# Last two expert quads' weight homes exchanged, last down weights in column halves, first unit of block 2 in row halves, router chain reordered

## The reference, cut to what matters

```
g_sel = argmax(xn @ w_router_group + b)             # 1 group of 4
top_v, top_i = top_k(e_logits of that group, 2)      # 2 of its 8 experts
gates = g_prob * softmax(top_v)
hdn = ragged_dot(xs, w_e_in, sizes)                  # 32 experts, 1024 x 512
act = silu(gate_h) * up_h
ys = ragged_dot(act, w_e_out, sizes)                 # 256 x 1024
h = h + scatter_add(ys * gates)
...
h = rms_norm(h, norm_f_g); xn = rmsnorm(h, ln1)      # block 2
proj = xn @ w_in_2                                   # first columns used: v_a, v_c, f, then q_a, k_a
```

## Time and profile before

| | us |
|---|---|
| three runs | 919.08, 919.75, 921.74; median 919.75 |
| the profiled execution, time | 920.25 |
| its span | 918.4 |
| TensorE busy | 836.1 (91%) |
| VectorE, ScalarE, POOL busy | 493.2, 385.9, 96.9 |
| DMA | 217.55 MB, mean 237 GB/s |

### The profile page before, as it was taken

One profiled execution on the slowest core, in us unless ns is written; L12 is line 12 of the kernel. 1 busy time (PEld: TensorE's weight loads), 2 busy tenths in 40 slices (PEclk: granted clock), 3 DMA queues, 4 the chain that ended last, 5 costly groups with the idle time before them and its releaser, 6 DMA issues.

```text
span 918.4 us, 14705 instructions
## 1 busy us (share of the span) xinstructions
PE 836.1 (91%) x5971; PEld 693.7 (76%) x5971; DVE 493.2 (54%) x768; ACT 385.9 (42%) x526; POOL 96.9 (11%) x115
## 2 busy tenths in 40 slices
PE   4989999999999996875678899999999899999996
PEld 4989789989997532322332599999997799999995
DVE  5898577764564411101110476555776577677584
ACT  5333454455332321111110665456554366556462
POOL 4322000111000000000000401122160000000000
PEclk9999999999999998988898999999999999999998
DMA  8665555234689999999999985434536446646511
GB/s 279 226 194 183 184 184 184 92 126 151 234 334 400 390 423 421 422 421 422 422 421 408 270 182 184 175 105 180 144 132 231 159 138 215 197 141 227 180 46 46
DMA packets 93647, 217.55 MB, mean 237 GB/s; under 512 B 13919, under 2 KB 44765, under 8 KB 81305
## 3 DMA queue, kind: packets, MB, share of 16 engines
q1 hardware_dynamic: 92905, 215.32, 64.9%
q10 hardware_dynamic: 576, 1.18, 0.4%
q0 software_dynamic: 112, 0.30, 0.3%
HBM read 215.44 MB, written 1.34 MB: 236 GB/s over the span
## 4 chain that ended last, share of the span: by engine, by line
PE 71%; DMA 13%; DVE 9%; ACT 3%; issue 2%; SPq 1%; POOL 0%; DVEq 0%; ACTq 0%
PE ps L858 17%; PE ps L859 16%; PE ps L860 16%; DMA moe_ring<-in_w_expert_in 12%; PE ps L1281 6%; PE ps L1197 6%; DVE w_lo L1658 3%; PE ps L1229 1%; PE ps L1219 1%; PE ps L1013 1%; PE ps L1023 1%; PE ps L1169 1%; DMA h_tok<-in_x 1%; SPq L724 1%; PE ps L1061 1%
## 5 line engine op out<-in xcount | busy, mean ns | idle before, releaser
L860 PE MATMUL ps<-x_hi,w_lo 128*128 128x256 f32 x664 | 189.1, 285 | 0.0
L860 PEld LDWEIGHTS ps<-x_hi,w_lo 128*128 128x128 f32 x664 | 128.7, 194 | 0.0
L1658 DVE TENSOR_TENSOR w_lo<-stage,w_hi 128x2048 fp32r<-128x2048 f32 (+1 forms) x44 | 101.8, 2354 | 25.3 <-ACT w_hi L1362 23.5
L858 PE MATMUL ps<-x_hi,w_hi 128*128 128x256 f32 x360 | 104.7, 291 | 4.7 <-DVE w_lo L1658 3.9
L859 PE MATMUL ps<-x_lo,w_hi 128*128 128x256 f32 x360 | 103.2, 287 | 0.0
L1362 ACT ACTIVATE w_hi<-stage 128x2048 fp32r<-128x2048 f32 (+1 forms) x44 | 79.2, 1849 | 55.7 <-PE ps L860 49.9
L858 PE MATMUL ps<-x_hi,w_odd 128*128 128x256 f32 x312 | 89.8, 288 | 1.3 <-DVE x_lo L1649 1.3
L859 PE MATMUL ps<-x_lo,w_odd 128*128 128x256 f32 x312 | 88.9, 285 | 0.0
L860 PE MATMUL ps<-x_hi,w_odd 128*128 128x256 f32 x312 | 88.9, 285 | 0.0
L858 PE MATMUL ps<-x_hi,w_lo 128*128 128x256 f32 x304 | 86.5, 285 | 0.0
L859 PE MATMUL ps<-x_lo,w_lo 128*128 128x256 f32 x304 | 86.0, 283 | 0.0
(11 more groups left out here) (386 smaller groups left out, 1914.7 us busy)
## 6 DMA issues: line engine op xcount, KB each, us to landing
stage<-in_w_in SPq DMA_DIRECT2D x23, 2048.0 KB, 8.1
moe_ring<-in_w_expert_in SPq DMA_DIRECT2D x44, 1024.0 KB, 18.3
moe_ring<-in_w_expert_out SPq DMA_DIRECT2D x20, 1024.0 KB, 15.7
stage_b<-in_w_up SPq DMA_DIRECT2D x12, 1024.0 KB, 7.6
stage<-in_w_down SPq DMA_DIRECT2D x11, 1024.0 KB, 5.2
stage<-in_w_up SPq DMA_DIRECT2D x10, 1024.0 KB, 9.6
up_odd<-in_w_expert_in SPq DMA_DIRECT2D x8, 1024.0 KB, 20.2
down_odd_a<-in_w_expert_out SPq DMA_DIRECT2D x6, 1024.0 KB, 21.7
```

The costliest lines, as they stand in the source:

```text
L858: mm(out, still[0], moving[0], start=first, stop=False)
L860: return mm(out, still[1], moving[0], start=False, stop=last)
L1658: tt(lo[:, cols], staged(n)[:, cols], hi[:, cols].bitcast(fp32), ALU.subtract).then_inc(lo_ready, 1)
```

## The change

1. Homes: up(6, half 1) goes to `up_odd` and up(7, half 0) to `moe_up[1]`, and they change places in SP's queue; down(7) goes to `up_odd`'s home. The semaphores that TensorE waits for follow.
2. Down(7) is loaded in two column halves, eight DMAs of 0.5 MB with 2 KB pieces, each half with a semaphore; the last quad's down products wait for their half. The last scatter goes (tile 0, half 0), (1, 0), (0, 1), (1, 1).
3. `vvf` is loaded in two row halves, six DMAs, and SP also waits for the last `up_full` ahead of it. POOL splits row half 0, ScalarE and VectorE row half 1; ScalarE's cast for it stands ahead of the norm, its first cast of `qka` behind the norm's `raw_hi`. `kbvb`'s load no longer waits for the last `down_b`, the bias loads do.
4. `route()`: the rank product of tile 0 and the first half of tile 1's logits ahead of the wait for the last quarter of h_tok; transposes copied in two halves; one rank product after `choose(1)` ahead of the signal; the sums for `most` after it, with a signal of their own; `residual`s moved. ScalarE scales tile 0 before it waits for the last quarter; POOL adds EPS ahead.

```diff
@@ -282,7 +282,7 @@
     u = units[s["unit"]]
-    s["pool"] = u["name"] == "vvf" or s["half"] == 1 and (u["name"], u["i"]) in POOL_SPLITS
+    s["pool"] = (u["name"], s["half"]) == ("vvf", 0) or s["half"] == 1 and (u["name"], u["i"]) in POOL_SPLITS
...
@@ -607,15 +608,20 @@
            for x in (down_odd_a, down_odd_b) for n in range(2)]
-down_last = [moe_up[1][:, j, :, :].rearrange("p k c -> p (k c)").rearrange("p (f c) -> p f c", c=D) for j in range(QUAD)]
+up_odd_home = [up_odd[:, 0, :, :], up_odd[:, 1, :, :], up_odd_c[:, :, :], up_odd_d[:, :, :]]
+down_last = [x.rearrange("p k c -> p (k c)").rearrange("p (f c) -> p f c", c=D) for x in up_odd_home]
...
-    if last and half == 1:
-        return up_last[j]
-    if (p, half) == (1, 0):
-        return up_odd[:, j, :, :] if j < 2 else (up_odd_c, up_odd_d)[j - 2][:, :, :]
-    return moe_up[half][:, j, :, :]
+    if (p, half) == (0, 0):
+        home = moe_up[0][:, j, :, :]
+    elif (p, half) == ((0, 1) if last else (1, 0)):
+        home = up_odd_home[j]
+    elif last and half == 1:
+        home = up_last[j]
+    else:
+        home = moe_up[1][:, j, :, :]
+    return home
...
@@ -655,9 +661,11 @@
             dst = staged3(n, WIDTH[name])
-            eng.dma_start(dst[:, :, 0:256], w_in2[:, :, VA0:VA0 + 256]).then_inc(first_in, 16)
-            eng.dma_start(dst[:, :, 256:384], w_in2[:, :, VC0:VC0 + 128]).then_inc(first_in, 16)
-            eng.dma_start(dst[:, :, 384:388], w_in2[:, :, FB0:FB0 + 4]).then_inc(first_in, 16)
+            for half in range(2):
+                ks = slice(half * KT // 2, (half + 1) * KT // 2)
+                eng.dma_start(dst[:, ks, 0:256], w_in2[:, ks, VA0:VA0 + 256]).then_inc(first_in[half], 16)
+                eng.dma_start(dst[:, ks, 256:384], w_in2[:, ks, VC0:VC0 + 128]).then_inc(first_in[half], 16)
+                eng.dma_start(dst[:, ks, 384:388], w_in2[:, ks, FB0:FB0 + 4]).then_inc(first_in[half], 16)
...
@@ -717,17 +725,24 @@
+    def up_landed(p, half, last):
+        if last and (p, half) == (1, 1):
+            return up_last_in
+        if last:
+            return moe_in[(4, 1)[p]]
+        return moe_in[4 if (p, half) == (1, 0) else half]
...
             src = w_up[half][:, e, :, :].rearrange("p e k n -> p (e k n)")
-            eng.dma_start(expert_up(p, half, j, last).rearrange("p k n -> p (k n)"), src).then_inc(up_last_in if last else moe_in[4 if (p, half) == (1, 0) else half], 16)
-
-    def load_down(q, p, experts=range(QUAD), last=False):
+            eng.dma_start(expert_up(p, half, j, last).rearrange("p k n -> p (k n)"), src).then_inc(up_landed(p, half, last), 16)
+
+    def load_down(q, p, experts=range(QUAD)):
...
             src = w_down[:, e, :, :].rearrange("p e f n -> p (e f n)")
-            eng.dma_start(expert_down(p, j, last).rearrange("p f n -> p (f n)"), src).then_inc(down_last_in if last else moe_in[2 + p], 16)
+            eng.dma_start(expert_down(p, j).rearrange("p f n -> p (f n)"), src).then_inc(moe_in[2 + p], 16)
...
@@ -744,10 +759,18 @@
         load_down(QUADS - 2, 0)
-        next_quad(QUADS // 2 - 2, 1)
+        eng.wait_ge(up_a, QUADS - 2 + it0)
+        load_up(QUADS - 2, 0, 1, last=True)
+        eng.wait_ge(up_full, QUADS - 2 + it0)
+        load_up(QUADS - 1, 1, 0, last=True)
+        eng.wait_ge(down_b, QUADS - 2 + it0)
...
         eng.wait_ge(up_full, QUADS - 1 + it0)
-        load_down(QUADS - 1, 1, last=True)
+        for half in range(2):
+            for j in range(QUAD):
+                cols = slice(half * BANK, (half + 1) * BANK)
+                e = QUADS * QUAD - QUAD + j
+                eng.dma_start(expert_down(1, j, True)[:, :, cols], w_down[:, e, :, cols]).then_inc(down_last_in[half], 16)
...
@@ -788,25 +811,24 @@
...
     for n in range(units_one, len(units)):
-        if n == units_one + STAGES:
+        if n == units_one + STAGES + 1:
             eng.wait_ge(down_b, passes * QUADS)
-        if n == units_one + STAGES + 1:
...
             eng.wait_ge(y_b, passes * QUADS)
+            eng.wait_ge(up_full, passes * QUADS)
...
@@ -1089,31 +1111,35 @@
-        residual(0, 0)
...
         eng.wait_ge(sel_ready, 1)
+        mm(ps[:, 1, 0:32], tri[:, 0:P], chosen[:, 0, :], start=True, stop=True).then_inc(rank_full, 1)
+        wait_read(eng, "at", "xt", 1)
+        router_logits(3, 1, range(0, 4))
...
         eng.wait_ge(h_ready, 4)
-        mm(ps[:, 2, 0:32], tri[:, 0:P], chosen[:, 0, :], start=True, stop=True).then_inc(rank_full, 1)
...
             last = eng.transpose(ps[:, 0, k * P:(k + 1) * P], interleaved(h_tok, 1, 1)[:, k, :], ident[:, :])
-        last.then_inc(xt_full, 1)
-        residual(0, 1)
-
-        wait_read(eng, "at", "xt", 1)
-        eng.wait_ge(xt_copied, 1)
-        router_logits(3, 1).then_inc(lg_full, 1)
+            if k % 2 == 1:
+                last.then_inc(xt_full, 1)
+        mm(ps[:, 2, 0:32], tri[:, P:S], chosen[:, 0, :], start=True, stop=False)
+
+        residual(0, 0)
+        for half in range(2):
+            eng.wait_ge(xt_copied, half + 1)
+            last = router_logits(3, 1, range(4 + 2 * half, 6 + 2 * half))
+        last.then_inc(lg_full, 1)
...
             gather_of(half, 0)
+        residual(0, 1)
...
         eng.wait_ge(sel_ready, 2)
-        mm(ps[:, 2, 32:64], tri[:, P:S], chosen[:, 0, :], start=True, stop=False)
-        mm(ps[:, 2, 32:64], tri[:, 0:P], chosen[:, 1, :], start=False, stop=True)
-        mm(ps[:, 2, 64:96], tri[:, P:S], chosen[:, 0, :], start=True, stop=False)
-        mm(ps[:, 2, 64:96], tri[:, P:S], chosen[:, 1, :], start=False, stop=True).then_inc(rank_full, 1)
+        mm(ps[:, 2, 0:32], tri[:, 0:P], chosen[:, 1, :], start=False, stop=True).then_inc(rank_full, 1)
+        for t in range(NT):
+            last = mm(ps[:, 3, 0:32], tri[:, P:S], chosen[:, t, :], start=(t == 0), stop=(t == 1))
+        last.then_inc(rank_full, 1)
...
@@ -1185,17 +1212,21 @@
             eng.wait_ge((xg_a, xg_b)[half], it + 1)
-            if half == 0:
+            if half == 0 and not final:
                 eng.wait_ge(moe_in[(0, 4)[p]], it * 32 + (64, 32)[p])
+            elif half == 0:
+                eng.wait_ge(moe_in[1], (r + 1) * (64 * (QUADS - 1)))
...
                 eng.wait_ge(up_last_in, r * 64 + 64)
+            elif tail:
+                eng.wait_ge(moe_in[4], it * 32 + 64)
...
                     last = mm(ps[CAP * j:CAP * (j + 1), 2, :], xg[p][:, k, CAP * j:CAP * (j + 1)],
-                              expert_up(p, half, j, final)[:, kk, :], start=(k == 0), stop=(k == KT - 1),
+                              expert_up(p, half, j, tail)[:, kk, :], start=(k == 0), stop=(k == KT - 1),
...
@@ -1207,13 +1238,13 @@
             eng.wait_ge(xg_b, it + 2)
-        if final:
-            eng.wait_ge(down_last_in, r * 64 + 64)
-        elif p == 0:
+        if p == 0:
             eng.wait_ge(moe_in[2], it * 32 + 64)
-        else:
+        elif not final:
...
         for half in range(2):
+            if final:
+                eng.wait_ge(down_last_in[half], r * 64 + 64)
...
@@ -1222,14 +1253,14 @@
         eng.wait_ge(spread_ready, it + 1)
-        for t in range(NT):
-            for half in range(2):
-                if t == 0:
-                    eng.wait_ge((y_a, y_b)[half], it + 2)
-                last = mm(ps[:, 4 + 2 * t + half, :], spread[:, t * P:(t + 1) * P],
-                          y_slots[:, half * BANK:(half + 1) * BANK], start=False, stop=False,
-                          skip_group_check=True)
-            last.then_inc((scat0, scattered)[t], 1)
+        for t, half in ((0, 0), (1, 0), (0, 1), (1, 1)) if final else ((0, 0), (0, 1), (1, 0), (1, 1)):
+            if t == 0:
+                eng.wait_ge((y_a, y_b)[half], it + 2)
+            last = mm(ps[:, 4 + 2 * t + half, :], spread[:, t * P:(t + 1) * P],
+                      y_slots[:, half * BANK:(half + 1) * BANK], start=False, stop=False,
+                      skip_group_check=True)
+            if half == 1:
+                last.then_inc((scat0, scattered)[t], 1)
...
@@ -1474,8 +1505,9 @@
-        half_square(1, 1)
         for t in range(NT):
+            if t == 1:
+                half_square(1, 1)
...
@@ -1575,17 +1607,19 @@
         if s["op"] == "split":
-            if s["unit"] == units_one + 1:
-                if s["half"] == 0:
-                    split(s["unit"], 0)
-            elif s["unit"] != units_one:
+            if s["unit"] not in (units_one, units_one + 1):
                 split(s["unit"], s["half"])
+            elif s["unit"] == units_one and s["half"] == 1:
+                eng.wait_ge(first_in[1], 16 * 3)
+                cols = slice(units[units_one]["size"] // 2, units[units_one]["size"])
+                act(split_pair(units_one)[0][:, cols], staged(units_one)[:, cols], ACT.Copy).then_inc(first_hi, 1)
...
             if s["i"] == 2:
+                split(units_one + 1, 0)
...
@@ -1652,7 +1686,10 @@
         u = units[n]
-        eng.wait_ge(hi_ready, hi_count(n, half))
```

(45 more changed lines are left out.)

## The result

| | before | after |
|---|---|---|
| median of six runs each, us | 919.41 | 914.72 (912.93 to 915.92) |
| ratio after / before | | 0.995, 95% interval 0.9933 to 0.9967 |
| profiled execution: time, span, us | 920.25, 918.4 | 915.7, 913.9 |

The change is 0.5% faster: 4.7 us by the medians and 4.5 us by the two spans, where 3.2 were forecast. The same kernel run again as e9_after_again has a ratio of 0.9951 (0.9929 to 0.9972).

A forecast was written before the change was run, and what follows sets the result against it. The weight stream bounds the expert stage, with 35 us of compute behind a misordered transfer. Products end at 507.0, plus 2.0 clock and 8.0 tail: 517.0 against 520.29; less 0.1, 3.2 us gained, 916.55 us, range 914.3 to 918.9.

The forecast's parts named there:

- Homes exchanged: Quads 6 and 7: up(6, half 1) lands earlier, TensorE neither waits nor loses clock; 9.5 us off the compute.
- Halves: Down(7) in column halves: landing takes 11.0 us instead of 10.2, but 1.8 us less product time behind it.
- Router: Router chain: quad 0 starts 1.0 us earlier, closing part of a stream hole; 0.7 us taken, bounds 0 and 1.0.
- Clock: Tail behind TensorE's 3.7 us wait for down(7): half clock costs 2.0 us, between 1.5 and 2.7.
- rival B: Clock holds behind the last down weights' wait: gain 5.2 us, 914.55 us; chance 0.15.
- Tail order and first unit: Last down products to first `vvf` product: 8.0 us instead of 6.8, giving back 1.2; POOL no longer holds it.
- Block 2 "moves as a whole": Second block: TensorE bound without a gap, so it shifts by the whole gain; 0.1 us charged for later `rstd2`.
- Rival C: Front of block 2 becomes the bound; late `rstd2`, `x_lo` or `qka` give 917.5 to 918.9 us; chance 0.2.
- D: Half-width down(7) DMAs miss 390 GB/s; gain gone at 14.2 us, median 922.3 at 250 GB/s; chance 0.05.
- E: No visible effect: stream's end sets block 2's start, needing `vvf` after 513; 919 to 920 us; chance 0.05.

The follow-up runs named there:

- e9_after_again: The changed kernel run again, unchanged: 915.90 us, ratio 0.9951.
- e1: Homes exchange alone on the kernel before, with SP's wait ahead of `vvf` and load order as changed: 919.01 us, ratio 1.0009.
- e2: Changed kernel, but down(7) in four whole DMAs behind one wait: 916.98 us, ratio 0.9975.
- e8: Changed kernel, two scatter products in the wait, `vvf` split behind the fourth `raw_lo`, whole tail by columns: 911.93 us, ratio 0.9928.
- e10: e8 with the router chain of the kernel before: 913.82 us, ratio 0.9943.
- e4: Changed kernel plus twelve filler products in TensorE's wait between the last down products' halves: 913.28 us, ratio 0.9945.
- e6: Changed kernel with the first unit as before: three DMAs, both halves split by POOL, ScalarE's old order: 919.46 us, ratio 1.0008.
- e11: Changed kernel plus one tiny VectorE operation ahead of the first split of unit `wo2` in block 2: median 914.17 us.
- e5: Changed kernel with two scatter products put into the wait between the last down products' halves: 915.16 us, ratio 0.9953.
- e7: Changed kernel with VectorE's split of `vvf` moved behind its second `raw_lo`: 914.56 us, ratio 0.9954.
- e3: Changed kernel with the router chain of the kernel before: 914.65 us, ratio 0.9961.

## Why the prediction was right, and where its terms were off

The time came inside the range, 1.8 us under the predicted 916.55. The first product was forecast at 517.0 and came at 516.75, but that is luck: the last weights landed 1.1 us earlier than forecast (504.07, not 505.2), and from there to the first product it took 12.7 us instead of 11.8. A third miss, 1.0 us, lies behind it.

- **Homes exchanged: right.** No wait at quad 6's second half, full clock, end at 480.03 (480.6 forecast, of which part is the earlier stream). But e1 shows that the exchange alone brings nothing. The steps gave it 9.5 us "off the compute"; I had not asked what would be late at the first unit.
- **Halves: landing right, saving not seen.** 10.8 us from 493.26 to 504.07 (11.0 forecast), one whole costs 10.0 to 10.2 (e1, e2). The page DMA: Bandwidth & Descriptors, Specifications, of the Trainium skill would have them free; here they cost 0.7. The forecast's 1.8 us less product time, net 1.0, did not appear in the profile it can be compared with: at half clock the whole (e2) reaches the first product at 516.77, the halves at 516.75. I had priced products and clock apart; in these two executions the longer wait had less slow work behind it. The halves are still worth 2.3 us in the times.
- **Router: mis-sized.** 0.7 taken, 1.0 given as the upper bound; measured 1.5 at quad 0 and 1.7 to 1.9 at the end (e8 against e10). The bound was the error. I set "some 1.0 us" at quad 0 from one hidden logits half and subtracted for `residual`, though several waits of the chain were shortened, and I capped the stream's share by that. In the profiled execution, with 0.3 us of chance ahead of the router, up(7, half 1) landed at 493.26 where 494.2 was forecast.
- **Clock: mechanism right, size and certainty off.** 2.0 taken, 2.7 measured, the upper bound of the forecast (e4: 4.74 against 7.45 us). The same 32 products at half clock in the earlier trace rows had said 2.7 for a burst of 3.6 us, and this tail is longer. And forecast and rival B are not rivals: the five profiles show both. The two groups of times, 3.0 us apart, suggest seven and six of 13 executions, but the clock near 48 and 718 us moves the times too. The gap of 2.65 us that the forecast set against B is itself one of these places: in four of 14 profiles the clock held behind it. The section "HAM oscillation — how this bites in real kernels" of TensorE: Matmul & The Clock Gate in the Trainium skill tells of waits of some 3 to 5 us for a DMA, with every next burst slow; behind the 3.24 to 3.37 us here that came in two of five traces.
- **Tail order and first unit: size right, reason wrong.** From the third scatter product to the first product of `vvf` 5.26 us were forecast (8.0 less 2.74) and 5.19 measured. The reason given for what is saved, that POOL "would have held it there", fell: the first product needs row half 0 only, and in e1 it started while POOL was busy. What would have held it is ScalarE's `qka` cast ahead of the norm. I had charged its move with 0.1 us; e6 shows that without that move and the split by rows together nothing of the gain is left. How much of the 4.7 us is each one's wasn't tried, nor was the scatter order by itself.
- **Block 2 "moves as a whole": wrong by 1.0 us, in the kernel's favour.** From the first product to the end the profile before took 398.1 us, after 397.1, with the clock fallen near 720 us in both. e11 shows the cause. Rival C had looked for losses there only; the slack it doubted was enough.
- **Rivals.** D, the narrow pieces, did not come (10.8 us, not 14.2); E did not either, though e1 and e6 show it one edit away. `vvf` landed at 509.43, under the 513 it needed.

## What to carry to other kernels

An edit that ends a stage earlier is worth only what the next stage's earliest in-order neighbour lets through. Look for operations that stand ahead of the critical one on its engine and wait for a load (here ScalarE's cast), and move them in the same edit. Filling a wait with work of the same chain pays once the whole tail goes by columns (e8); one link at a time only moved the wait, and the half clock with it (e5, e7). Where a wait is long enough to lower the clock in some executions, compare means and groups, not medians of six, and before two profiles are compared read the clock at every wait of both: part of what they differ by can lie there and not in the edit (e3, e4).

## What the runs showed of the hardware

- The clock behind a wait of TensorE can differ from execution to execution. Behind 3.24 to 3.37 us, with the same order of work, it was half in two profiles and full in three; up to VectorE's scaling the price was 2.7 to 2.9 us. Waits of 4.74 and 5.09 us (e2, e1) brought it both times. Shorter ones brought it too, but not always: behind 2.14 us in e6 the up products of quad 7, half 1, took 5.38 us, behind 2.82 us in e3 they took 3.69.
- VectorE's split of two SBUF operands and POOL's product of two SBUF operands shut each other out for a whole operation, and the first to start wins. 0.23 us later cost VectorE 1.0 us. The Trainium skill says so: in SBUF — State Buffer, "SBUF: two separate sides", the pair of ports that both use is an exclusive lock. The traces agree with it (3.30 and 3.35 against 2.32 us; 2.22 against 1.76 where the split of `vvf` met POOL's, e4), and it would have been the page to ask about block 2.
- Down weights in 2 KB pieces alone, 4 MB in 10.8 us, ran at 388 GB/s, in 8 KB pieces (10.0 to 10.2 us) at 411 to 419. The first came in eight DMAs, the second in four; no run tells the two apart.
